# Four input-projection units instead of six kept for the boundary between output projection and MLP, in a fused two-layer hybrid trunk

## What is computed

```python
def even_mixer(h, S0, conv_buf, w_in, ...):
    proj = h @ w_in
    qkv, gate, beta_pre, a_pre, u_pre, v_pre = split_cols(proj, (CONV_CH, V_A, H_A, H_A, W_B, W_B))
    qkv_c, new_buf = short_conv(qkv, conv_buf, conv_w)
    ...
    o, S = gated_delta_rule(q, k, v, g, beta, S0)
    o_a = rmsnorm(o, gdn_norm_g) * jax.nn.silu(gate...)
    u = jax.nn.gelu(u_pre, approximate=False)
    vb = rmsnorm(jax.nn.gelu(v_pre, approximate=False), sgu_norm_g)
    o_b = spatial_gating(u, vb, sgu_w, sgu_b)
    out = jnp.concatenate([o_a, o_b], -1) @ w_out
...
x = x + rmsnorm(mix, gl[1])
h = rmsnorm(x, gl[2])
x = x + rmsnorm(squared_relu_mlp(h, w_ff1[l], w_ff2[l]), gl[3])
```

## Time and profile before

| | us |
|---|---|
| median of 3 runs | 2748.53 (2748.27 to 2750.63) |
| the profiled execution | 2745.14 |
| its span, first to last instruction | 2743.2 |
| PE busy | 2686.4 (98%) |
| DVE busy | 1369.3 (50%) |
| ACT busy | 1161.9 (42%) |
| POOL busy | 218.4 (8%) |

### The profile page before, as it was taken

How to read it: one execution, slowest core, us unless ns; L and a number is a source line. 1 busy time by engine, 2 the same in 40 slices (tenths; PEclk the granted TensorE clock), 3 DMA queues, 4 the chain that set the end, 5 groups by cost and what they waited for, 6 DMA issues and landing times.

```text
span 2743.2 us, 40845 instructions
## 1 busy us (share of the span) xinstructions
PE 2686.4 (98%) x17050; PEld 2392.1 (87%) x17050; DVE 1369.3 (50%) x2157; ACT 1161.9 (42%) x2017; POOL 218.4 (8%) x354
## 2 busy tenths in 40 slices
PE   7999999999999999999999999999999999999999
PEld 5789897888888779889999998998877797999998
DVE  4645654654554446543443456444454447444334
ACT  5554446554544335433334335434432344333334
POOL 5110001100000000110000000110010000000000
PEclk9999999999999999999999999999999999999999
DMA  6442323522323234654333325544444334233232
GB/s 187 155 142 83 90 71 111 163 70 85 93 70 94 78 108 147 192 152 121 92 101 105 100 74 160 181 127 144 129 130 131 108 103 139 89 105 108 93 92 79
DMA packets 366566, 315.71 MB, mean 115 GB/s; under 512 B 11261, under 2 KB 339003, under 8 KB 366384
## 3 DMA queue, kind: packets, MB, share of 16 engines
q1 hardware_dynamic: 336224, 207.91, 25.9%
q0 software_dynamic: 30160, 105.20, 12.0%
HBM read 258.12 MB, written 54.94 MB: 114 GB/s over the span
## 4 chain that ended last, share of the span: by engine, by line
PE 87%; DVE 5%; ACT 5%; issue 1%; DMA 1%; SPq 0%; POOL 0%; DVEq 0%; ACTq 0%
PE dense L552 75%; PE mixer L552 10%; ACT arena L1074 1%; DVE wlo L1584 1%; ACT whi L1074 1%; DVE hf L1722 1%; PE mixer L791 1%; DMA proj<-ffh 0%; DVE hlo L1718 0%; ACT ffh L1074 0%; ACT relu L1074 0%; ACT hhi L1074 0%; DMA arena<-in_x_prompt_dram 0%; PE mixer L923 0%; PE mixer L995 0%
## 5 line engine op out<-in xcount | busy, mean ns | idle before, releaser
L552 PE MATMUL dense<-hhi,whi 128*128 128x272 f32 (+1 forms) x3072 | 854.8, 332 | 16.9 <-DVE hlo L1718 8.5
L552 PE MATMUL dense<-hhi,wlo 128*128 128x272 f32 (+1 forms) x3072 | 827.8, 324 | 0.0
L552 PE MATMUL dense<-hlo,whi 128*128 128x272 f32 (+1 forms) x3072 | 826.0, 323 | 0.0
L1584 DVE TENSOR_TENSOR wlo<-wst,whi 128x1024 fp32r<-128x1024 f32 x384 | 469.7, 1223 | 244.4 <-ACT whi L1074 243.5
L552 PEld LDWEIGHTS dense<-hhi,whi 128*128 128x128 f32 x3072 | 516.5, 189 | 77.8 <-issue 15.3
L1074 ACT ACTIVATE whi<-wst 128x1024 fp32r<-128x1024 f32 x384 | 404.0, 1052 | 405.2 <-PE dense L552 400.6
L552 PEld LDWEIGHTS dense<-hhi,wlo 128*128 128x128 f32 x3072 | 514.7, 189 | 42.8
L552 PEld LDWEIGHTS dense<-hlo,whi 128*128 128x128 f32 x3072 | 517.1, 189 | 37.2 <-issue 1.0
L552 PE MATMUL dense<-h1hi,whi 128*128 128x272 f32 (+1 forms) x1536 | 424.3, 330 | 11.1 <-DVE wlo L1584 6.0
L552 PE MATMUL dense<-h1lo,whi 128*128 128x272 f32 (+1 forms) x1536 | 413.9, 324 | 0.0
L552 PE MATMUL dense<-h1hi,wlo 128*128 128x272 f32 (+1 forms) x1536 | 413.4, 323 | 0.0
(11 more groups left out here) (323 smaller groups left out, 1857.6 us busy)
## 6 DMA issues: line engine op xcount, KB each, us to landing
wst<-in_w_ff_dram SPq DMA_DIRECT2D x256, 512.0 KB, 3.9
wst<-in_w_in_even_dram SPq DMA_DIRECT2D x48, 512.0 KB, 3.8
wst<-in_w_in_odd_dram SPq DMA_DIRECT2D x48, 512.0 KB, 3.8
proj<-ffh POOLq DMA_DIRECT2D x48, 272.0 KB, 2.4
proj<-ffh POOLq DMA_DIRECT2D x48, 256.0 KB, 2.3
arena<-proj POOLq DMA_DIRECT2D x16, 512.0 KB, 4.6
wst<-in_w_out_even_dram SPq DMA_DIRECT2D x16, 512.0 KB, 4.0
arena<-proj POOLq DMA_DIRECT2D x8, 1024.0 KB, 7.8
```

Of the source, the lines that this page charges most:

```text
L552: return pe.matmul(out, lhsT, rhs, start=start, stop=stop)
L1584: TT(wlo[:, u % 2, :], wst[:, u % 2, :], whi[:, u % 2, :].bitcast(F32), ALU.subtract)\
```

## The change

Blocks 14 and 15 go from the held units to the first stage, and the order of blocks 11, 12 and 13 at the end of that stage is plain. The first stage then has 20 units (80 pieces, the side list mixed over 77), and 4 units are held. The number of units, their contents and the side lists stay as they are. The norms' 20 items are mixed over 12 pieces in place of 20. The count at line 2325 follows the length of `SEQ_1` and goes from 21 to 22 stores.

```diff
 SEQ_A = [20, 21, 22, 0, 1, 2, 3, 4, 5, 6, 7, 8, 9, 10, 11, 23]
 SEQ_B = list(range(12, 20))
-SEQ_1 = [0, 20, 1, 2, 21, 3, 4, 22, 5, 6, 7, 23, 8, 9, 10, 12, 11, 13]
-SEQ_2 = [14, 15, 16, 17, 18, 19]
+SEQ_1 = [0, 20, 1, 2, 21, 3, 4, 22, 5, 6, 7, 23, 8, 9, 10, 11, 12, 13, 14, 15]
+SEQ_2 = [16, 17, 18, 19]
 
 SEQ_3 = list(range(16, NCH)) + list(range(16))
```

## The result

The change made the kernel slower by a little: the ratio of its time to the time before is 1.0019, 95% interval 1.0013 to 1.0025, from 20 runs of each (medians 2756.26 and 2750.67 us). On 2748.53, the median of three runs that the prediction started from, that is +5.2 us (3.6 to 6.9), 2753.8 for a forecast of 2753.2.

A forecast was written before the change was run, and what follows sets the result against it. TensorE, with an instruction in flight for 98% of the span, was taken to bound the kernel. First stage +7.5, boundary -3.3 and clock +0.5 gave +4.7 on 2748.53: 2753.2 us, range 2746.5 to 2759.

The forecast's parts named there:

- The first stage: Beside the delta rule: two more units cost 12.04 us plus 0.6, less healed waits; +7.5 us, bounds 6.0 and 9.5.
- the pairs: First stage: items sharing one piece part, giving back 1.5 us, and 0.6 more for lb(6) with zw.
- the table changes: First stage, ACT: units 14 and 15 bring two more table changes of 1.28 us; 0.3 reaches TensorE.
- The time of the sum: Norm sum 3 at the boundary: DVE's chain sets it; last addition starts 3.8 us earlier, sum matmul at 511.2.
- the rival in which the units paced the norm: Boundary: DVE's chain, held up by interleaving, shrinks with the units and gives back nearly 12 us; total -4.5; chance 0.07.
- From the sum to the MLP's second unit: Boundary behind norm sum 3: chunks end 0.5 us later, between 0.3 earlier and 1.7 later; clock adds 0.5.
- the order: ACT behind norm sum 3: first rounding now stands behind unit 19's evacuation and table change; 0.5 us later.
- the clock: TensorE's wait at norm sum 3 brings its clock down earlier, slowing the MLP's matmuls: +0.5 us, ends 0 and 3.
- The slower rival: Norm sum 3: half clock lasts, unit 19's last piece delays evacuation and rounding; +7.6 us, 2756; chance 0.40 with all over +5.5.
- the equal rival: First stage: all 7.8 us of waits and 1.7 of pairs heal; total -1.3, 2747 us; chance 0.08.
- The longer table change: ACT at the boundary: the skill's 2.66 us per change against 1.28 seen; chunks another 1.4 later, 2754.6 us.
- the faster rival: Boundary gives back nearly 12 us, -4.5 in total; with the output projection's stall healed, -7.5, 2741 us; chance 0.07.

The follow-up runs named there:

- the filler: The changed kernel with 24 matmuls, results overwritten, on TensorE ahead of its wait at norm sum 3; ratio 1.0016 to the kernel before, boundary 48.2 us.
- both edits together: The changed kernel with 24 overwritten matmuls before norm sum 3 and the first rounding ahead of unit 19's evacuation on ACT; ratio 1.0009 to the kernel before.

## Why the prediction was right

The sign and the mechanism were right: TensorE arrives early, DVE's chain sets the time of the sum, and little comes back. The size was near (+4.7 for +5.2), but by the stages the change cost +6.5, so the terms were short by 1.8 together, and that the timed figure lies within 0.5 of the forecast is in part luck. The terms one by one:

- **The first stage**: +7.5 forecast, +8.4 measured. Before any healing the two units and their interruptions were to cost 12.64; the healing was 4.3 and not 5.1. The waits were to come down to 4.1 by the terms (three of 1.0 at L779, 1.1 at L840) and are 4.8: L779 has 0.8 more, L840 fell to 0.3 against the forecast, L1844 kept 0.3, and L766 and L1850 add 0.4. The terms for the pairs and the table changes were not measured one by one.
- **The time of the sum**: 31.9 after the first held unit was forecast (511.2 - 479.27), 31.7 measured; 2.06 a chunk forecast, 2.07 measured. The standstill was to be 7.3 in one piece; it is 7.0 in two, since the weight split of unit 19, which I had counted in DVE's chain, has a waiter of its own. This step carries the prediction: the rival in which the units paced the norm would have brought the sum 12 us earlier, and it came 4 us earlier.
- **From the sum to the MLP's second unit**: 17.0 + 0.5 for the order + 0.5 for the clock was forecast (the boundary 49.4, and 49.9 with the clock), 19.0 measured (50.7). This is the term that was mis-sized. I laid the clock on the MLP's matmuls, which the chunks cover, and they were covered but for 0.3. It was paid ahead of them: the filler shows 2.0 for the clock in place of 0.5. The order costs nothing while the clock is up (17.0 with five held units) and 0.7 while it is down, and those 0.7 do not come on top of the 2.0, since both edits together still leave 16.8. The slower rival named this path, the last piece at half clock holding the evacuation, and took 2.7 for it. Neither condition by which it was to decide came true: the half clock ended at 538.3, ahead of the end of the MLP's first unit at 540.1, and the wait at L1844 shrank to 0.3.
- **A slip in a sum**: the upper bound of what the boundary gives back is 3.8 + 0.3 = 4.1 and not 4.4, so the least of the sum is +1.9 and the equal rival ends at -1.0. The forecast itself does not hang on it.
- **What stays uncertain**: the sum of the stages is +6.5, the timed +5.2 with an interval to 6.9. The page of the Trainium skill that warns of gaps between bursts ("TensorE: Matmul & The Clock Gate", "Why this matters for your kernels") is borne out by 0.72 and 0.58 behind the wait and 1.00 with the filler; its price here was the 2.0 that the filler gave back. The longer table change that the prediction prices beside its sum is not seen: in the changed kernel the activation at 526.77 starts 0.01 behind the end of the load.
- The equal rival (all latency heals) failed at L779, which the order of the items keeps. The output projection, whose stall was to vanish in the faster rival, did not change.

## What to carry to other kernels

Work held back to cover a chain on another engine is worth its full time only up to the length of that chain. Compare when the covering engine arrives with when the chain is done: with six units held TensorE waits 0.6 for a sum at 35.7, with five 1.8 for one at 33.5, with four 7.0 in all for one at 31.7. The chain is not of fixed length, since each held unit brings a weight split of 1.2 that can lie in it. A unit beyond the chain costs about the same on either side; a unit below it is lost in the wait, and here the longer wait also cost 2.0 by the clock. Where latency seems to heal by spreading items out, look at which waits are between neighbours in the list; those stay however thin the list is spread, and moving the awaited operation forward on its engine may only hand the wait on.

## What the runs showed of the hardware that I had not expected

- The clock fell to half in the first stage in some executions and not in others of the same program, and often with no wait ahead of it. In 199.59 to 210.00 of the second profile of the kernel before, TensorE is busy for 10.41 of 10.41, and in 210.00 to 214.10 the clock is 0.58. The first profile of the same program has no fall in this stage. Each fall cost 1.6 us. Seven of the thirteen profiles had one to four, sixteen in all; five of these lie in a wait of 1.9 to 2.7 or within 1.2 us behind it, and the other eleven have no wait over 0.5 in the 5 us ahead of them. So a difference of a few us between two profiles says nothing until the falls are taken off.
- An fp32 matmul of 128 columns is recorded as two, which start 0.11 us apart (48 records in 5.52 us), so filling work for a given time needs half as many calls as one would count from the records.
- A wait of 2.1 us at a norm sum (six held units, sum asked early) was followed by a half-clock stretch at 515.3, while a wait of 1.8 at the same place with five held units was not. That is no limit, though: the wait of 2.4 at L779 was followed by a fall in the second profile of the kernel before and not in the first.
